# Other start places within 256 bytes for the split tokens of each layer norm

## The chip, the cores and the metric

The kernel runs on one core of a Trainium2 chip. The metric is the device time of one execution in microseconds (us); lower is better.

## The reference, cut to what matters

Two post-norm decoder layers over 256 tokens of width 2048, all in float32. Layer 0 mixes tokens with sliding-window attention (window 128, sinks, relative-position bias), layer 1 with forgetting attention; after each mixer comes a gated MLP of width 5632 with a causal convolution of width 3.

```python
def reference(x, ...):
    for i in range(DEPTH):                       # DEPTH = 2
        y = swa_sink_attention(...) if i % 2 == 0 else forgetting_attention(...)
        x = layer_norm(ALPHA * x + y, ln_g[i, 0], ln_b[i, 0])
        y = conv_ffn(x, ffn_w_up[i], ffn_conv_w[i], ffn_conv_b[i], ffn_w_down[i])
        x = layer_norm(ALPHA * x + y, ln_g[i, 1], ln_b[i, 1])
    return x

def conv_ffn(x, w_up, conv_w, conv_b, w_down):
    h = x @ w_up
    h = lax.conv_general_dilated(h, ...) + conv_b
    g, u = h[..., :D_FF], h[..., D_FF:]
    return (jax.nn.silu(g) * u) @ w_down
```

The change touches nothing of what is computed.

## The kernel before, in words

**The products.** Every large product is made of three matmuls in the rounded float32 form: both operands are split into a rounded high part and a low remainder, and high by low, low by high and high by high are added up in PSUM. Tokens in turned form (128 of the 2048 features on the partitions, 256 tokens along the row) lie in `xh` (high) and `xl` (low), 16 tiles of 1024 bytes a partition each. Weights come in chunks of 128x1024 through a ring of four: SyncE issues the load into `raw`, ScalarE copies it into `w_hi` (L473), VectorE subtracts into `w_lo` (L751), TensorE uses it.

**Two forms.** `turned_product` (L1171 to L1183) keeps 128 weight columns stationary and moves the 256 tokens of a row of `xh` or `xl` past them: its three matmuls are L1178 (`w_lo`, moving `xh`), L1180 (`w_hi`, moving `xl`) and L1181 (`w_hi`, moving `xh`), for four groups of columns. `turned_first` (L1185, matmuls L1191) does the same for the first row after a layer norm. `product` (L1155 to L1169, matmuls L1164 to L1166) keeps 128 tokens stationary and moves 512 weight columns. The turned form makes queries, keys and the up projections; the other form makes the values, the output projections (from `oh`, `ol`) and the down projections (from `hid_h`, `hid_l`). The decay gate of layer 1 has a product of its own at L1414 to L1416: 32 weight columns of `wf_lo` or `wf_hi` stationary, `xh` or `xl` moving.

**Order of the stages.** Mixer 0 (keys and values first, then four groups of queries with attention woven in), output projection, layer norm, MLP 0 (11 pairs of up projections, then down), layer norm, mixer 1 (four groups of queries, keys and values), output projection, layer norm, MLP 1, last layer norm. The instruction streams of all engines are written out by hand; semaphores tie them. `xh` and `xl` are written four times, once for each index `xi`: 0 is the input (used by mixer 0), 1 the norm before MLP 0, 2 the norm before mixer 1, 3 the norm before MLP 1. `xt_turn` (transposes L1255 and L1260 with `ident` moving) brings a tile into PSUM, `xt_evacuate` of ScalarE (L505, L508, L523) writes `xh`, and `xt_evacuate` of VectorE (L783, L786, L792) writes `xl`. `keep_clock` (L1239) is a run of matmuls of `ident` with itself that bridges each norm. No DMA reads or writes `xh` or `xl`.

**Where tiles lie.** SBUF tiles lie one behind another in the order of their allocation, each start rounded up to a multiple of 32 bytes. `res`, `raw`, `w_hi`, `w_lo`, `tok`, `cg`, `cu`, `xh`, `xl`, `oh`, `ol`, `bias`, `qT`, `kz`, `vv`, `prob`, `hid_h` and `hid_l` all start at a multiple of 256 bytes, so each row of `xh` and `xl` (1024 bytes) and each column group of `w_hi` and `w_lo` (512 bytes) does too. Some tiles do not: `ident` starts 128 bytes past a multiple of 256; `wf`, `wf_hi` and `wf_lo` start 192 bytes past one; the nine `fs` tiles of the decay (`fs0` to `fs8`) start 224 bytes past one. `xh` starts at byte 104448 of the partition, `xl` at 120832. `lnfull`, the scales of the last norm, lies on the same bytes as `xh`; `xh_hold` reserves them.

Of the kernel before, what the change touches and what calls it, by code (L numbers as in the profile page):

```python
# [22 lines left out]
F32R = mybir.dt.float32r  # L23
# [3 lines left out]
P = 128  # L27
D = 2048
SEQ = 256
MT = SEQ // P  # L30
DEPTH = 2
HD = 64
HEADS = D // HD
# [5 lines left out]
KT = D // P  # L39
# [20 lines left out]
KC = KT // 2  # L60
FC = FT // 2
CH_A_KV = 0
# [12 lines left out]
TURN_A_KV = 0  # L75
# [48 lines left out]
def trunk(nc, x, a_w_qkv, a_w_o, a_sinks, rel_bias, b_w_qkvf, b_f_bias, b_w_o,  # L124
          ffn_w_up, ffn_conv_w, ffn_conv_b, ffn_w_down, ln_g, ln_b, out):
    ctx = ExitStack()
    with ctx:
        def sb(name, shape, dt=FP32, where=ctx):
            return where.enter_context(nc.sbuf_tensor(name, shape, dt))
# [25 lines left out]
        convcol = sb("convcol", [P, DEPTH, 4, 2 * FT])  # L155
        sb("fill_to_xh", [P, 320])
        with ExitStack() as first:
            xh = sb("xh", [P, KT, SEQ], F32R, first)
        with ExitStack() as later:
            lnfull = sb("lnfull", [P, 2, D], FP32, later)  # L160
        xh_hold = sb("xh_hold", [P, KT * SEQ])
        xl = sb("xl", [P, KT, SEQ], F32R)
        with ExitStack() as mix:
            oh = sb("oh", [P, KT, SEQ], F32R, mix)
            ol = sb("ol", [P, KT, SEQ], F32R, mix)
# [20 lines left out]
            cumq = sb("cumq", [P, MT, HEADS], FP32, mix)  # L186
        hid_h = sb("hid_h", [P, FT, SEQ], F32R)
        hid_l = sb("hid_l", [P, FT, SEQ], F32R)
        ps = ctx.enter_context(nc.psum_tensor("ps", [P, 8, COLS], FP32))
        S_BANK, O_BANK, PT_BANK, X_BANK = 4, 6, 7, 4  # L190
        FIRST_BANK, AGAIN_BANK = X_BANK + 3, X_BANK + 2
# [13 lines left out]
        v_tile0 = sem("v_tile0")  # L205
# [250 lines left out]
        def _(act):  # L456
# [39 lines left out]

            def xt_evacuate(xi, l, s, g):

                if xi == 0:
                    act.wait_ge(xt_turned, g + 1)  # L500
                    src = ps[:, X_BANK + g % 4, :].rearrange("p (a t) -> p a t", a=2)
                else:
                    if g == 0:
                        act.wait_ge(first_turned, xi)
                        act.activation(xh[:, 0, :], ps[:, FIRST_BANK, 0:SEQ], ACT.Identity,  # L505
                                       scale=lncol[:, 0, l, s, 0:1], bias=lncol[:, 1, l, s, 0:1]).then_inc(first_high, 1)
                        act.wait_ge(xt_turned, KC * xi + 1)
                        act.activation(xh[:, 1, :], ps[:, X_BANK, SEQ:2 * SEQ], ACT.Identity,  # L508
                                       scale=lncol[:, 0, l, s, 1:2], bias=lncol[:, 1, l, s, 1:2]).then_inc(xt_high, 1)
                        return  # L510
                    src = cg[:, 2 * (g % 2):2 * (g % 2) + 2, :]
                    if g in DVE_FULL:
                        act.wait_ge(xt_full, FULLS * (xi - 1) + DVE_FULL.index(g) + 1)
                    else:

                        act.wait_ge(xt_low, KC * xi + g - 1)
                        act.wait_ge(xt_turned, KC * xi + g + 1)
                        for a in range(2):
                            k = 2 * g + a
                            last = act.activation(cg[:, 2 * (g % 2) + a, :], ps[:, X_BANK + g % 4, a * SEQ:(a + 1) * SEQ],  # L520
                                                  ACT.Identity, scale=lncol[:, 0, l, s, k:k + 1], bias=lncol[:, 1, l, s, k:k + 1])
                        own.link(last)
                act.activation(xh[:, 2 * g:2 * g + 2, :], src, ACT.Copy).then_inc(xt_high, 1)  # L523
# [216 lines left out]
        def _(dve):  # L740
# [33 lines left out]

            def xt_evacuate(xi, l, s, g):

                if xi == 0:
                    src = ps[:, X_BANK + g % 4, :].rearrange("p (a t) -> p a t", a=2)
                elif g == 0:
                    first_tile(xi, l, s, 0)  # L780
                    dve.wait_ge(first_full, xi)
                    dve.wait_ge(first_high, xi)
                    dve.tensor_tensor(xl[:, 0, :], cg[:, 0, :], xh[:, 0, :].bitcast(FP32), ALU.subtract).then_inc(first_low, 1)  # L783
                    first_tile(xi, l, s, 1)
                    dve.wait_ge(xt_full, FULLS * (xi - 1) + 1)
                    dve.tensor_tensor(xl[:, 1, :], cg[:, 1, :], xh[:, 1, :].bitcast(FP32), ALU.subtract).then_inc(xt_low, 1)  # L786
                    return
                else:
                    src = cg[:, 2 * (g % 2):2 * (g % 2) + 2, :]
                high = xh[:, 2 * g:2 * g + 2, :].bitcast(FP32)  # L790
                dve.wait_ge(xt_high, KC * xi + g + 1)
                dve.tensor_tensor(xl[:, 2 * g:2 * g + 2, :], src, high, ALU.subtract).then_inc(xt_low, 1)  # L792
# [363 lines left out]
        def _(pe):  # L1156
            def product(s, turn, k, nk, lh, ll, slot, tile0=None, tiles=range(MT)):
# [10 lines left out]
                        last.then_inc(tile0, 1)  # L1168
                return last  # L1169

            def turned_product(s, turn, k, slot):  # L1171

                for j in range(4):
                    if k == 0 and j % 2 == 0:
                        pe.wait_ge(acc_free[s][j // 2], turn)
                    cols = slice(j * P, (j + 1) * P)
                    o = ps[:, 2 * s + j // 2, (j % 2) * SEQ:(j % 2 + 1) * SEQ]
                    pe.matmul(o, w_lo[:, slot, k % 2, cols], xh[:, k, :], start=(k == 0 and j % 2 == 0), stop=False,  # L1178
                              skip_group_check=True)
                    pe.matmul(o, w_hi[:, slot, k % 2, cols], xl[:, k, :], start=False, stop=False, skip_group_check=True)  # L1180
                    last = pe.matmul(o, w_hi[:, slot, k % 2, cols], xh[:, k, :], start=False, stop=(k == KT - 1),  # L1181
                                     skip_group_check=True)
                return last  # L1183

            def turned_first(s, turn, slot, xi):  # L1185

                def parts(w, xs, start=False):
                    for j in range(4):
                        if start and j % 2 == 0:
                            pe.wait_ge(acc_free[s][j // 2], turn)  # L1190
                        pe.matmul(ps[:, 2 * s + j // 2, (j % 2) * SEQ:(j % 2 + 1) * SEQ], w[:, slot, 0, j * P:(j + 1) * P],  # L1191
                                  xs[:, 0, :], start=start and j % 2 == 0, stop=False, skip_group_check=True)
                pe.wait_ge(first_high, xi)
                parts(w_lo, xh, True)
                parts(w_hi, xh)
                pe.wait_ge(first_low, xi)
                parts(w_hi, xl)
# [15 lines left out]
                        last.then_inc(chunks_used, 1)  # L1213
                    yield k

            def group(s, turn, b4, loc0, lh=xh, ll=xl, nk=KT, before=None, tile0=None):

                for k in range(nk):
                    loc = loc0 + k // 2
                    if k % 2 == 0:  # L1220
                        if before:
                            before(k // 2)
                        pe.wait_ge(low_ready, b4 * 4 + (loc + 1))
                    if tile0 is last_tile0 and k >= nk - 2:

                        if k == nk - 1:
                            for m in range(MT):
                                for kk in (k - 1, k):
                                    last = product(s, turn, kk, nk, lh, ll, loc % RING, tile0, (m,))
                    else:  # L1230
                        last = product(s, turn, k, nk, lh, ll, loc % RING, tile0)
                    if k % 2 == 1:
                        last.then_inc(chunks_used, 1)
                    yield k
# [29 lines left out]
            def x_ready(xi):  # L1264
                def before(c):
                    if c == 0:
                        keep_clock(1.7 if xi == 0 else 3.4)
                        xt_turn(xi, 0)
                        xt_turn(xi, 1)
                        if xi:  # L1270
                            return
                    pe.wait_ge(xt_low, KC * xi + c + 1)
                return before
# [84 lines left out]
                    yield slot  # L1358

            def mixer_a():  # L1360
                for k in group(0, TURN_A_KV, CH_A_KV // 4, 0, before=x_ready(0)):
                    x_next(0, k)
                for k in turned_group(1, TURN_A_Q[1], CH_A_Q // 4, 0):
                    if k == 1:
# [26 lines left out]

            def mixer_b():
                t0, t1 = TURN_B

                def woven(k, n):

# [6 lines left out]
                def turn(n, b4, first=False):  # L1403
# [14 lines left out]
                    for k in turned_group(1, n + t1, b4, KC):  # L1418
                        if first and k == 12:
# [2 lines left out]
                                last = pe.transpose(ps[:, 7, m * HEADS:(m + 1) * HEADS], fs[7][:, m * P:(m + 1) * P],  # L1422
                                                    ident[0:HEADS, 0:HEADS])
                            last.then_inc(cum_turned, 1)
                    for k in group(0, n * 2 + (t0 + 1), b4, 2 * KC, tile0=v_tile0):
                        pass

                turn(0, CH_B // 4, first=True)
# [10 lines left out]

            def mlp(l):  # L1440
                t0, t1 = TURN_UP[l]

                def turn(n, b4, first=False):
                    for k in turned_group(0, n + t0, b4, 0, before=x_ready(1 + 2 * l) if first else None,
# [9 lines left out]
                with pe.Fori(0, OUT_GROUPS // 2) as n:  # L1454
                    for i in range(2):
                        for k in group(i, n + TURN_DOWN[l][i], n * (2 * FC // 4) + CH_DOWN[l] // 4, i * FC, hid_h, hid_l, FT,
                                       tile0=last_tile0 if i == 1 else None,
                                       before=lambda c: pe.wait_ge(hid_low, UP_PAIRS * (l + 1) - (1 if c < FC - 2 else 0))
# [37 lines left out]
```

## Time and profile before

| what | value |
|---|---|
| median of 2 runs | 2239.07 us (2239.05 to 2239.08) |
| profiled execution, its own time | 2239.63 us |
| its span, first to last instruction | 2237.8 us |
| TensorE matmuls busy | 2207.8 us (99%), 15265 matmuls |
| VectorE, ScalarE, GpSimd busy | 1337.7, 1038.4, 217.1 us |
| mean DMA rate | 183 GB/s |

The profiled execution lasts 1.8 us longer than its span. Busy time of TensorE counts matmuls that overlap once. Two matmuls that follow each other overlap in the profile, so the time that one costs is read from the distance of two starts, or from the busy time of a stretch divided by its matmuls, and not from its own duration.

### The profile page before, as it was taken

The page shows a single profiled execution, that of the slowest core. Times are in us where ns is not written, and L with a number is a line of the kernel's source. Part 1 is how long each engine was busy: PE and PEld are TensorE (multiplying, and loading weights), DVE is VectorE, ACT ScalarE, POOL GpSimd, SP SyncE. Part 2 cuts the span into 40 slices and gives each one's busy share as a digit, 9 for nine tenths or more (in the row PEclk, how much of TensorE's full clock was granted, in tenths as well). Part 3 has the DMA queues.
Part 4 walks back from the last instruction along what each step waited for, and adds up shares of the span by engine and source line. Part 5 has one row for each costly group of instructions (what it writes and reads, how often), then busy time and mean ns, then how long its engine had stood idle before and what let it go on. Part 6 is the DMA issues. An engine that isn't in the chain of part 4 may idle for free.

```text
span 2237.8 us, 40894 instructions
## 1 busy us (share of the span) xinstructions
PE 2207.8 (99%) x15265; PEld 2061.6 (92%) x15265; DVE 1337.7 (60%) x1805; ACT 1038.4 (46%) x1380; POOL 217.1 (10%) x206
## 2 busy tenths in 40 slices
PE   9999999999999999999999999999999999999996
PEld 8998899999999988888999998899999999988885
DVE  5566676665666554546665565576666566554445
ACT  4554464454444443335444444364444444443332
POOL 2000002220000000000240330001230000000001
PEclk9999999999999999999999999999999999999998
DMA  8444556666666666655655654656666666666653
GB/s 263 148 147 159 178 170 198 190 194 182 183 180 185 179 193 192 195 190 163 189 182 163 201 169 141 204 155 196 193 199 182 180 185 179 185 225 191 194 193 109
DMA packets 206953, 408.71 MB, mean 183 GB/s; under 512 B 12653, under 2 KB 13757, under 8 KB 206621
## 3 DMA queue, kind: packets, MB, share of 16 engines
q1 hardware_dynamic: 200192, 385.92, 56.8%
q0 software_dynamic: 5776, 21.34, 3.0%
q8 instruction: 49, 0.80, 0.1%
q10 hardware_dynamic: 908, 0.43, 0.1%
q14 instruction: 28, 0.22, 0.0%
HBM read 405.46 MB, written 2.18 MB: 182 GB/s over the span
## 4 chain that ended last, share of the span: by engine, by line
PE 96%; DVE 3%; ACT 0%; issue 0%; DMA 0%; DVEq 0%; ACTq 0%
PE ps L1178 19%; PE ps L1181 19%; PE ps L1180 19%; PE ps L1164 11%; PE ps L1166 11%; PE ps L1165 11%; PE ps L1306 1%; PE ps L1313 1%; PE ps L1325 1%; PE ps L1324 1%; PE ps L1305 1%; DVE w_lo L751 1%; PE ps L1323 0%; PE ps L1255 0%; DVE cg L796 0%
## 5 line engine op out<-in xcount | busy, mean ns | idle before, releaser
L751 DVE TENSOR_TENSOR w_lo<-raw,w_hi 128x1024 fp32r<-128x1024 f32 x728 | 922.5, 1273 | 672.7 <-ACT w_hi L473 671.1
L473 ACT ACTIVATE w_hi<-raw 128x1024 fp32r<-128x1024 f32 x728 | 770.3, 1058 | 999.7 <-PE ps L1181 582.5
L1178 PE MATMUL ps<-xh,w_lo 128*128 128x256 f32 x3572 | 1020.0, 286 | 2.5 <-DVE xl L792 1.5
L1181 PE MATMUL ps<-xh,w_hi 128*128 128x256 f32 x3572 | 1010.6, 283 | 0.0
L1180 PE MATMUL ps<-xl,w_hi 128*128 128x256 f32 x3572 | 1010.5, 283 | 0.0
L1178 PEld LDWEIGHTS ps<-xh,w_lo 128*128 128x128 f32 x3572 | 685.0, 192 | 5.4 <-DVE xl L792 2.9
L1180 PEld LDWEIGHTS ps<-xl,w_hi 128*128 128x128 f32 x3572 | 685.2, 192 | 0.3
L1181 PEld LDWEIGHTS ps<-xh,w_hi 128*128 128x128 f32 x3572 | 685.0, 192 | 0.0
L1164 PE MATMUL ps<-w_lo,hid_h 128*128 128x512 f32 x704 | 273.9, 389 | 0.0
L1165 PE MATMUL ps<-w_hi,hid_l 128*128 128x512 f32 x704 | 273.9, 389 | 0.0
L1166 PE MATMUL ps<-w_hi,hid_h 128*128 128x512 f32 x704 | 273.9, 389 | 0.0
L1166 PEld LDWEIGHTS ps<-w_hi,hid_h 128*128 128x128 f32 x704 | 132.1, 188 | 27.7
L1165 PEld LDWEIGHTS ps<-w_hi,hid_l 128*128 128x128 f32 x704 | 132.1, 188 | 27.3
L1164 PEld LDWEIGHTS ps<-w_lo,hid_h 128*128 128x128 f32 x704 | 132.1, 188 | 27.2
L395 POOL COPY cw<-convcol 128x16 f32 (+1 forms) x40 | 41.9, 1048 | 801.8 <-DVE cu L1080 441.3
L1164 PE MATMUL ps<-w_lo,oh 128*128 128x512 f32 x256 | 102.4, 400 | 0.0
L1166 PE MATMUL ps<-w_hi,oh 128*128 128x512 f32 x256 | 99.9, 390 | 0.0
L1165 PE MATMUL ps<-w_hi,ol 128*128 128x512 f32 x256 | 99.7, 390 | 0.0
L1080 DVE SCALAR_TENSOR_TENSOR cu<-ps,cw,cu 128x254 f32<-128x254 f32 (+1 forms) x176 | 76.6, 477 | 1.6
L1080 DVE SCALAR_TENSOR_TENSOR cg<-ps,cw,cg 128x254 f32<-128x254 f32 (+1 forms) x176 | 76.5, 476 | 1.6
L1164 PE MATMUL ps<-w_lo,xh 128*128 128x512 f32 x160 | 63.7, 398 | 2.6 <-issue 2.6
L1165 PE MATMUL ps<-w_hi,xl 128*128 128x512 f32 x160 | 63.1, 394 | 0.0
(164 smaller groups left out, 1497.1 us busy)
## 6 DMA issues: line engine op xcount, KB each, us to landing
raw<-in_ffn_w_up_dram SPq DMA_DIRECT2D x352, 512.0 KB, 3.6
raw<-in_ffn_w_down_dram SPq DMA_DIRECT2D x176, 512.0 KB, 4.6
raw<-in_b_w_qkvf_dram SPq DMA_DIRECT2D x96, 512.0 KB, 4.4
raw<-in_a_w_qkv_dram SPq DMA_DIRECT2D x40, 512.0 KB, 4.4
raw<-in_a_w_o_dram SPq DMA_DIRECT2D x32, 512.0 KB, 4.3
raw<-in_b_w_o_dram SPq DMA_DIRECT2D x32, 512.0 KB, 4.6
bias<-rel_by_distance POOLq DMA_DIRECT2D x4, 1024.0 KB, 6.4
bias<-minus_cumulated_decay POOLq DMA_DIRECT2D x4, 1024.0 KB, 6.4
```

The source lines that it names most:

```text
L395: gp.tensor_copy(cw[:, h], convcol[:, l, :, bass.ds(n * 4 + h * FT, 4)]).then_inc(cw_ready, 1)
L473: act.activation(w_hi[:, loc % RING], raw[:, loc % RING], ACT.Copy).then_inc(high_ready, 1)
L751: dve.tensor_tensor(w_lo[:, s], raw[:, s], w_hi[:, s].bitcast(FP32), ALU.subtract).then_inc(low_ready, 1)
L1080: last = dve.scalar_tensor_tensor(dst[:, j, lag:SEQ], src, cw[:, h, tap, j:j + 1], dst[:, j, lag:SEQ], ALU.mult, ALU.add)
L1164: pe.matmul(o, lh[:, k, rows], w_lo[:, slot, k % 2, :], start=(k == 0), stop=False)
L1165: pe.matmul(o, ll[:, k, rows], w_hi[:, slot, k % 2, :], start=False, stop=False)
L1166: last = pe.matmul(o, lh[:, k, rows], w_hi[:, slot, k % 2, :], start=False, stop=(k == nk - 1))
L1178: pe.matmul(o, w_lo[:, slot, k % 2, cols], xh[:, k, :], start=(k == 0 and j % 2 == 0), stop=False, skip_group_check=True)
L1180: pe.matmul(o, w_hi[:, slot, k % 2, cols], xl[:, k, :], start=False, stop=False, skip_group_check=True)
L1181: last = pe.matmul(o, w_hi[:, slot, k % 2, cols], xh[:, k, :], start=False, stop=(k == KT - 1), skip_group_check=True)
L1305: pe.matmul(o[:, 0:P], qT[:, s // 2, 0:P], kz[:, kt, s % 2, 0:P], start=True, stop=True)
L1306: pe.matmul(o[:, P:SPAN], qT[:, s // 2, P:SEQ], kz[:, kt, s % 2, :], start=True, stop=True).then_inc(scores_ready, 1)
```

## The change

`xh` and `xl` become 256 bytes longer, and each layer norm's tokens start at a place of their own in them: 48, 8, 32 and 16 elements, which is 192, 32, 128 and 64 bytes, for `xi` 0, 1, 2 and 3. Both tiles use the same place for one `xi`. Every reader and writer takes the view of its `xi`. The rows keep their distance of 1024 bytes, so each row of one `xi` starts at the same place within 256 bytes. `xl` moves up by 256 bytes and all tiles behind it by 512. The number, order and shape of the instructions and their waits stay.

```diff
@@ -28,6 +28,10 @@
 MT = SEQ // P
+
+
+PLACES = (48, 8, 32, 16)
+PLACED = D // P * SEQ + 64
 DEPTH = 2
@@ -155,11 +159,11 @@
         with ExitStack() as first:
-            xh = sb("xh", [P, KT, SEQ], F32R, first)
+            xh_all = sb("xh", [P, PLACED], F32R, first)
         with ExitStack() as later:
             lnfull = sb("lnfull", [P, 2, D], FP32, later)
-        xh_hold = sb("xh_hold", [P, KT * SEQ])
-        xl = sb("xl", [P, KT, SEQ], F32R)
+        xh_hold = sb("xh_hold", [P, PLACED])
+        xl_all = sb("xl", [P, PLACED], F32R)
@@ -186,6 +190,7 @@
+        xhs, xls = ([t[:, at:at + KT * SEQ].rearrange("p (k t) -> p k t", t=SEQ) for at in PLACES] for t in (xh_all, xl_all))
@@ -496,6 +501,7 @@
             def xt_evacuate(xi, l, s, g):
 
+                xh = xhs[xi]
@@ -774,6 +780,7 @@
             def xt_evacuate(xi, l, s, g):
 
+                xh, xl = xhs[xi], xls[xi]
@@ -1168,7 +1175,11 @@
+            layer = [0]
+
             def turned_product(s, turn, k, slot):
+
+                xh, xl = xhs[layer[0]], xls[layer[0]]
@@ -1183,6 +1194,8 @@
             def turned_first(s, turn, slot, xi):
+
+                xh, xl = xhs[xi], xls[xi]
@@ -1213,7 +1226,7 @@
-            def group(s, turn, b4, loc0, lh=xh, ll=xl, nk=KT, before=None, tile0=None):
+            def group(s, turn, b4, loc0, lh, ll, nk=KT, before=None, tile0=None):
@@ -1358,7 +1371,7 @@
-                for k in group(0, TURN_A_KV, CH_A_KV // 4, 0, before=x_ready(0)):
+                for k in group(0, TURN_A_KV, CH_A_KV // 4, 0, xhs[0], xls[0], before=x_ready(0)):
@@ -1391,6 +1404,8 @@
             def mixer_b():
                 t0, t1 = TURN_B
+                layer[0] = 2
+                xh, xl = xhs[2], xls[2]
@@ -1422,7 +1437,7 @@
-                    for k in group(0, n * 2 + (t0 + 1), b4, 2 * KC, tile0=v_tile0):
+                    for k in group(0, n * 2 + (t0 + 1), b4, 2 * KC, xh, xl, tile0=v_tile0):
@@ -1439,6 +1454,7 @@
             def mlp(l):
                 t0, t1 = TURN_UP[l]
+                layer[0] = 1 + 2 * l
```

## Rows read from the trace of the kernel before

**Rows 1.** The page: span, busy time of the engines, granted clock in 40 slices.

```profile
span 2237.8 us, 40894 instructions
PE 2207.8 (99%) x15265; PEld 2061.6 (92%) x15265; DVE 1337.7 (60%) x1805; ACT 1038.4 (46%) x1380; POOL 217.1 (10%) x206
...
PEclk9999999999999999999999999999999999999998
```

**Rows 2.** The page: the chain that ended last, by engine.

```profile
PE 96%; DVE 3%; ACT 0%; issue 0%; DMA 0%; DVEq 0%; ACTq 0%
```

**Rows 3.** Stretches: stretch, busy us and count of each engine, granted clock, DMA share.

```profile
36.90:172.60 135.70, 135.70 (x1122) 133.45 (x1120) 82.39 (x211) 67.40 (x166) 5.27 (x6) 1.00 0.52 162
...
274.20:282.30 8.10, 7.29 (x48) 6.28 (x46) 6.87 (x21) 4.28 (x9) 0.33 (x2) 1.00 0.05 18
282.30:790.60 508.30, 507.75 (x4232) 507.35 (x4230) 323.12 (x383) 253.26 (x297) 52.98 (x44) 1.00 0.64 186
790.60:1030.00 239.40, 239.40 (x1059) 198.21 (x1058) 120.25 (x111) 97.41 (x94) 0.00 (x0) 1.00 0.61 193
...
1038.10:1360.70 322.60, 320.81 (x2312) 301.74 (x2311) 199.47 (x308) 151.54 (x240) 82.63 (x54) 1.00 0.59 182
...
1470.20:1978.50 508.30, 507.75 (x4231) 507.35 (x4230) 321.72 (x383) 253.23 (x297) 53.13 (x44) 1.00 0.64 186
```

**Rows 4.** Instruction groups: count | busy us, mean ns | idle before, releaser.

```profile
L1178 PE MATMUL ps<-xh,w_lo 128*128 128x256 f32 x3572 | 1020.0, 286 | 2.5 <-DVE xl L792 1.5 <-DVE vv L1043 0.9
...
L473 ACT ACTIVATE w_hi<-raw 128x1024 fp32r<-128x1024 f32 x728 | 770.3, 1058 | 999.7 <-PE ps L1181 582.5 <-PE ps L1166 374.2 <-DMA raw<-in_ffn_w_down_dram 16.0
...
L1164 PE MATMUL ps<-w_lo,xh 128*128 128x512 f32 x160 | 63.7, 398 | 2.6 <-issue 2.6
...
L1191 PE MATMUL ps<-xh,w_lo 128*128 128x256 f32 x12 | 2.1, 300 | 0.0
```

**Rows 5.** Timeline, mixer 1: start us, us; weights at 0, then at 192.

```profile
1062.15 0.28 PE L1178 MATMUL ps<-xh,w_lo 128*128 128x256 f32 x1
...
1062.27 0.28 PE L1180 MATMUL ps<-xl,w_hi 128*128 128x256 f32 x1
...
1062.51 0.28 PE L1414 MATMUL ps<-xh,wf_lo 128*32 128x256 f32 x1
...
1062.63 0.28 PE L1415 MATMUL ps<-xl,wf_hi 128*32 128x256 f32 x1
...
1063.19 0.28 PE L1414 MATMUL ps<-xh,wf_lo 128*32 128x256 f32 x1
```

**Rows 6.** Timeline of TensorE: plain float32 matmuls, `kz` (0) or `ident` (128) moving.

```profile
71.67 0.60 PE L1306 MATMUL ps<-kz,qT 128*128 128x256 f32 x2
...
274.24 3.62 PE L1239 MATMUL ps<-ident 128*128 128x256 f32 x16
```

**Rows 7.** Those two lines by themselves: count: duration ns min/median/max.

```profile
L1306 PE MATMUL ps<-kz,qT x128: 379/380/382, 67.5 to 1385.2; 128*128 128x256 f32 x128
...
L1239 PE MATMUL ps<-ident x56: 377/379/796, 1.5 to 1465.4; 128*128 128x256 f32 x56
```

**Rows 8.** Instruction groups, columns as Rows 4: the same work at 0, 192 and 224.

```profile
L792 DVE TENSOR_TENSOR xl<-cg,xh 128x512 fp32r<-128x512 f32 x21 | 14.5, 690 | 5.4 <-ACT xh L523 5.2
...
L523 ACT ACTIVATE xh<-cg 128x512 fp32r<-128x512 f32 x21 | 13.3, 633 | 14.2 <-DVE cg L796 13.9
...
L783 DVE TENSOR_TENSOR xl<-cg,xh 128x256 fp32r<-128x256 f32 x3 | 1.3, 425 | 0.1
...
L1049 DVE TENSOR_TENSOR wf_lo<-wf,wf_hi 128x512 fp32r<-128x512 f32 x1 | 0.7, 687 | 0.0
...
L638 ACT ACTIVATE wf_hi<-wf 128x512 fp32r<-128x512 f32 x1 | 0.6, 615 | 0.0
...
L1029 DVE TENSOR_TENSOR fs<-fs 32x256 f32<-32x256 f32 x1 | 0.4, 416 | 0.0
```

## The prediction

> **What bounds the kernel now.** I read the page first. Matmuls fill 2207.8 of the 2237.8 us of the span, the granted clock is at 0.9 or more in 39 of the 40 slices, and no other engine passes 60% [rows 1]. The chain that ended last is TensorE for 96% of the span [rows 2]. The groups say why the others are idle: of the 999.7 us that ScalarE sat idle before its copies into `w_hi`, 956.7 us were ended by a matmul that gave back a ring slot [rows 4]. The weights are ready early and the split engines wait for TensorE. So the time is the sum of matmuls times what each costs, and the change can only matter through (a) the cost of a matmul that reads `xh` or `xl`, (b) the writes of these tiles in the norms, (c) anything that the move of the other tiles does.
>
> The cost of a matmul comes from the stretches. The up projections of MLP 0 hold 4232 matmuls in 507.75 us, which is 0.1200 us each; those of MLP 1 give 507.75 / 4231 = 0.1200 as well. The down projections hold 1059 in 239.40 us, 0.2261 each [rows 3]. A moving row of 256 columns costs 0.1200 and one of 512 costs 0.2261, so 256 columns more cost 0.1061 us and the fixed part of a turned matmul is 0.1200 - 0.1061 = 0.0139 us. I keep 0.0139 as the piece of each turned matmul that does not stream columns.
>
> **The change part by part.**
>
> The moving reads. Each of L1178, L1180 and L1181 has 3572 matmuls, and L1191 has 12 for each of its three operand pairs (the one row shown has 12), so 3 x 3584 = 10752 turned matmuls move a row of `xh` or `xl` [rows 4]. By the loops they fall on the places as: 768 at 192 bytes (mixer 0), 4224 at 32 bytes (MLP 0), 1536 at 128 bytes (mixer 1) and 4224 at 64 bytes (MLP 1). 48 more are those of the decay gate, at 128 bytes. The trace has no matmul of the rounded form whose moving row starts off a multiple of 256 bytes, so the cost must be bounded.
>
> - Nearest row for "nothing": a 256-column matmul in plain float32 that moves `ident`, 128 bytes past a multiple of 256, against one that moves `kz`, at a multiple. Sixteen of the first last 3.62 us, one alone 0.379, so the pace is (3.62 - 0.38) / 15 = 0.216 us; two of the second last 0.60, so 0.60 - 0.38 = 0.22 us [rows 6, 7]. The same columns and weights, another place, the same pace to the rounding of the row. It reads a column in twice the time of the rounded form (0.216 against 0.120), so it leaves room to hide a small cost, and does not settle the case.
> - Lower end: the decay gate's matmuls move `xh` at the same pace of columns and run at (1063.19 - 1062.51) / 6 = 0.1133 us, against 0.120 just before them [rows 5]. Their stationary operand starts at 192 bytes and has 32 columns, not 128. If it is the place that helps, a turned matmul could fall by 0.0067 us: 10752 x 0.0067 = 72 us less.
> - Upper end: the plain float32 pace of 0.216 [rows 6], as if an odd start halved the read: 10752 x 0.096 = 1032 us more.
>
> Between ends so far apart I take zero, by the `ident` row, which is the only one that changes the place of a moving operand and little else.
>
> A rule bears on this. The Trainium skill (SBUF — State Buffer, Specifications) says that SBUF is read in lines of 16 bytes and that crossing to a new line is what costs. All four places are multiples of 16, so a row of 1024 bytes stays at 64 lines, and by that page the term is zero too; a place of 8 bytes would be another matter. No row here shows the line size.
>
> The stationary reads. 480 matmuls of the other form (three lines of 160, the first shown) take 128 tokens of `xh` or `xl` as weights while `w_lo` or `w_hi` moves, and these still move from a multiple of 256 [rows 4]. Stationary operands at an odd place are shown: `wf_lo` and `wf_hi` at 192, with no sign of a price (0.1133, below the usual pace) [rows 5]. I take zero; even the whole fixed part again, 480 x 0.0139, would be 6.7 us.
>
> The writes. ScalarE's and VectorE's evacuations of `xh` and `xl` have twins in the trace that work on `wf`, `wf_hi` and `wf_lo` at 192 bytes, with the same shape and types: 615 ns against 633 for ScalarE, 687 against 690 for VectorE; a two-input VectorE operation on 256 columns takes 416 ns on `fs` at 224 bytes (on 32 partitions) and 425 at a multiple of 256 [rows 8]. So an odd place costs these engines nothing to 0.02 us. There are 29 evacuations of each kind of 512 columns, and all but the first of each norm lie beside matmuls of the norm; the bridge of a norm is 8.1 us long with 7.29 us of matmuls in it [rows 3]. Taken at the largest difference seen, 0.018 us, two evacuations on the path of each of four fillings come to 0.14 us, either way. I take zero.
>
> The move of the other tiles. `xl` moves by 256 bytes, what lies behind it by 512. Each tile keeps its place within 256 bytes. The instructions, their order and waits are the same, so no queue and no wait changes. Zero. `lnfull` shares `xh`'s bytes as before and is loaded after the last up projection.
>
> The sum: 0 + 0 + 0 + 0. Against the profiled execution (span 2237.8, its own time 2239.63) that is 2239.6 us. The runs without a profile have a median of 2239.07, 0.56 below it, and agree within 0.03, so I predict 2239.1 us.
>
> **The rivals.**
>
> Slower: a block more for each moving row. A row of 1024 bytes that starts at a multiple of 256 lies in four blocks of 256 bytes; at any of the four new places it lies in five. If TensorE fetches by such blocks, the fifth takes the time of 64 columns, 0.1061 / 4 = 0.0265 us. Part of it may fit in the fixed 0.0139 us, where no columns stream; the rest, 0.0126, or with a less lucky overlap the 0.0139 again, is paid by each of 10752 matmuls: 10752 x 0.0139 = 149 us, which gives 2388.6 us. In full it would be 285 us, 2524 us. The point from which this decides is 44.8 us (2%, about what a measurement of this kernel can tell from no change) over 10752 matmuls, 0.0042 us each: ten columns' time. For it: every moving row of the rounded form now starts at a multiple, so the trace cannot deny it, and the read runs at twice the pace of plain float32. Against: L1239 reads the 512 bytes of `ident` twice from 128, each time three blocks in place of two, and shows nothing. The Trainium skill (DMA: Bandwidth & Descriptors, How a descriptor splits into AXI transactions) has just this rule of 256-byte blocks, but for a DMA; no DMA touches these tiles, and nothing here shows that TensorE follows it.
>
> Slower at one place alone. If blocks are of 64 bytes, only 32 is off (MLP 0): 4224 x 0.0139 = 59 us, 2297.8 us. If 192 bytes alone is bad, mixer 0 pays 768 x 0.0139 = 10.7 us, 2249.8 us, which is within 2%.
>
> Faster: a clash goes. The fixed part could be two reads, weights and tokens, that begin on the same place within 256 bytes; the matmuls with weights at 192 are 0.0067 quicker. All turned matmuls would have them apart after the change: 2239.1 - 72 = 2167 us. For it: the numbers just named. Against: those also load 32 columns of weights instead of 128, which explains a shorter fixed part as well; and `ident` loads and moves from the same place (128) at the pace of `kz` and `qT` [rows 6], while a clash should hit the former no less. In mixer 0 alone it would be 768 x 0.0067 = 5.1 us, 2234.0 us.
>
> The change does not do what it says: if the places ended up all alike within 256 bytes, the time stays, which can't be told from the forecast by time alone.
>
> **How the numbers follow.** No effect beyond 0.1%, 0.84. The fifth block in all layers 0.04; a price at one or two places of over 2% in total 0.02; a price at some place within 2% 0.04; the clash gone in all layers 0.03, in part 0.03 (of which 0.01 beyond 2%). Faster by over 2%: 0.04. Slower by over 2%: 0.06. Within 2%: 0.90. The range reaches to the two partial cases of mixer 0, 2234 below and 2250 above; beyond it lie the full rivals, and what they leave out is under 2 in 10.
>
> **What would show it.** Right: 4232 matmuls of MLP 0 in 507.8 us and the like number of MLP 1 in the same time, 0.1200 each, the down projections at 0.2261, evacuations at 633 and 690 ns. The fifth block: up projections at 0.134 or more, all alike in layers 0 and 1, down projections unchanged. One place: the stretches of mixer 0, MLP 0, mixer 1 and MLP 1 come out with different costs per matmul; that is what makes this change easy to read, since each has a place of its own. The clash: 0.113 in the turned form. If TensorE's pace stays and the time moves, the norms' bridges (8.1 us) have grown, and I mis-sized the writes.

## The result, and the profile after

The change takes the median from 2239.07 to 2213.94 us (2213.89 and 2213.99 in two runs): a ratio of 0.9888, 95% interval 0.9845 to 0.9930. It is faster, by 1.1%: clear of the noise, though within 2%, and outside the range, whose lower end was 2234. The profiled execution has a span of 2212.1 us against 2237.8, so 25.7 us less.

The page of the kernel after the change, its span, busy times, granted clock and last chain (lines of the code have moved: L1178, L1180, L1181 are now L1189, L1191, L1192; L1164 to L1166 are L1171 to L1173; L473 is L478):

```profile
span 2212.1 us, 40894 instructions
PE 2182.2 (99%) x15265; PEld 2033.5 (92%) x15265; DVE 1335.3 (60%) x1805; ACT 1039.1 (47%) x1380; POOL 217.7 (10%) x206
...
PEclk9999999999999999999999999999999999999998
...
PE 96%; DVE 3%; ACT 0%; DMA 0%; issue 0%; SPq 0%; ACTq 0%; DVEq 0%
```

Against [rows 1, 2] the instructions and the clock are the same, TensorE is still on 96% of the chain, and VectorE, ScalarE and GpSimd are busy within 2.4 us of what they were. TensorE's rows are what changed: its matmuls are busy for 25.6 us less, which is all of the gain, and its weight loads (PEld) for 28.1 us less. The stretches of the same stages say in which of them (the columns of [rows 3]):

```profile
36.60:169.30 132.70, 132.70 (x1122) 130.37 (x1120) 82.37 (x211) 67.31 (x166) 5.27 (x6) 1.00 0.52 166
...
270.90:279.00 8.10, 7.26 (x48) 6.26 (x46) 6.87 (x21) 4.27 (x9) 0.33 (x2) 1.00 0.06 24
279.00:773.40 494.40, 493.78 (x4231) 493.38 (x4229) 322.57 (x383) 253.58 (x297) 52.83 (x44) 1.00 0.65 191
773.40:1012.80 239.40, 239.40 (x1058) 198.23 (x1057) 120.21 (x111) 97.41 (x94) 0.00 (x0) 1.00 0.61 193
...
1020.90:1344.30 323.40, 321.91 (x2314) 300.75 (x2313) 197.07 (x308) 151.60 (x240) 82.60 (x54) 1.00 0.59 182
...
1453.70:1952.80 499.10, 498.50 (x4232) 498.10 (x4230) 322.74 (x383) 253.57 (x297) 53.99 (x44) 1.00 0.65 189
```

The up projections of MLP 0 (tokens at 32 bytes) lose 13.9 us, those of MLP 1 (64 bytes) 9.2 us, mixer 0 (192 bytes) 3.0 us, and mixer 1 (128 bytes) gains nothing: it is 0.8 us longer. The norm's bridge (8.1 us) and the down projections (239.4 us) are where they were. Per matmul, MLP 0 is at 493.78 / 4231 = 0.1167 us and MLP 1 at 498.50 / 4232 = 0.1178, against 0.1200 in both before.

The groups show that the engines that write these tiles did not feel the places (633 and 690 ns, as in [rows 8]), and that ScalarE's wait for ring slots got shorter by as much as TensorE did (999.7 us before, 974.2 now):

```profile
L1189 PE MATMUL ps<-xh,w_lo 128*128 128x256 f32 x3572 | 1007.2, 282 | 2.2 <-DVE xl L799 1.6
...
L478 ACT ACTIVATE w_hi<-raw 128x1024 fp32r<-128x1024 f32 x728 | 771.2, 1060 | 974.2 <-PE ps L1192 557.6 <-PE ps L1173 375.6 <-DMA raw<-in_ffn_w_down_dram 15.5
...
L799 DVE TENSOR_TENSOR xl<-cg,xh 128x512 fp32r<-128x512 f32 x21 | 14.5, 690 | 5.4 <-ACT xh L529 5.2
...
L529 ACT ACTIVATE xh<-cg 128x512 fp32r<-128x512 f32 x21 | 13.3, 633 | 14.2 <-DVE cg L803 13.9
```

So a turned matmul became cheaper, by an amount that depends on where the tokens start. Why the start should matter, and the start against what, is what the experiments were for.

### The profile page after: what moved, and what is told of

The parts are those of the page before. It is cut to its first block, busy times and chain, and to the rows that moved or that the text cites. A ratio compares the mean times of both kernels' runs of the same rounds, so it can differ in the third digit from the quotient of the medians.

```text
span 2212.1 us, 40894 instructions
## 1 busy us (share of the span) xinstructions
PE 2182.2 (99%) x15265; PEld 2033.5 (92%) x15265; DVE 1335.3 (60%) x1805; ACT 1039.1 (47%) x1380; POOL 217.7 (10%) x206
## 4 chain that ended last, share of the span: by engine, by line
PE 96%; DVE 3%; ACT 0%; DMA 0%; issue 0%; SPq 0%; ACTq 0%; DVEq 0%
PE ps L1192 19%; PE ps L1189 19%; PE ps L1191 19%; PE ps L1171 11%; PE ps L1173 11%; PE ps L1172 11%; PE ps L1319 1%; PE ps L1326 1%; PE ps L1338 1%; PE ps L1337 1%; PE ps L1318 1%; PE ps L1336 0%; DMA raw<-in_a_w_qkv_dram 0%; DVE cg L803 0%; PE ps L1345 0%; PE ps L1268 0%
## 5 line engine op out<-in xcount | busy, mean ns | idle before, releaser
L478 ACT ACTIVATE w_hi<-raw 128x1024 fp32r<-128x1024 f32 x728 | 771.2, 1060 | 974.2 <-PE ps L1192 557.6
L1189 PE MATMUL ps<-xh,w_lo 128*128 128x256 f32 x3572 | 1007.2, 282 | 2.2 <-DVE xl L799 1.6
L1192 PE MATMUL ps<-xh,w_hi 128*128 128x256 f32 x3572 | 999.0, 280 | 0.0
L1191 PE MATMUL ps<-xl,w_hi 128*128 128x256 f32 x3572 | 997.4, 279 | 0.0
L1189 PEld LDWEIGHTS ps<-xh,w_lo 128*128 128x128 f32 x3572 | 670.7, 188 | 5.2 <-DVE xl L799 3.0
L1191 PEld LDWEIGHTS ps<-xl,w_hi 128*128 128x128 f32 x3572 | 672.0, 188 | 0.4
L1192 PEld LDWEIGHTS ps<-xh,w_hi 128*128 128x128 f32 x3572 | 671.4, 188 | 0.0
L1171 PE MATMUL ps<-w_lo,hid_h 128*128 128x512 f32 x704 | 273.9, 389 | 0.0
L1173 PE MATMUL ps<-w_hi,hid_h 128*128 128x512 f32 x704 | 273.9, 389 | 0.0
L1173 PEld LDWEIGHTS ps<-w_hi,hid_h 128*128 128x128 f32 x704 | 132.2, 188 | 27.4
L1171 PEld LDWEIGHTS ps<-w_lo,hid_h 128*128 128x128 f32 x704 | 132.2, 188 | 27.4
L1171 PE MATMUL ps<-w_lo,oh 128*128 128x512 f32 x256 | 102.4, 400 | 0.0
L1173 PE MATMUL ps<-w_hi,oh 128*128 128x512 f32 x256 | 99.9, 390 | 0.0
L1171 PE MATMUL ps<-w_lo,xh 128*128 128x512 f32 x160 | 64.2, 401 | 3.1 <-issue 2.6
L1173 PE MATMUL ps<-w_hi,xh 128*128 128x512 f32 x160 | 63.6, 398 | 0.0
```

Source lines behind the costliest of these rows:

```text
L478: act.activation(w_hi[:, loc % RING], raw[:, loc % RING], ACT.Copy).then_inc(high_ready, 1)
L1171: pe.matmul(o, lh[:, k, rows], w_lo[:, slot, k % 2, :], start=(k == 0), stop=False)
L1173: last = pe.matmul(o, lh[:, k, rows], w_hi[:, slot, k % 2, :], start=False, stop=(k == nk - 1))
```

## The experiments

Each kernel is the changed one with other places. `xh` and `xl` get places of their own, and where weights move too, `w_hi` and `w_lo` become 256 bytes longer and begin at a place as well, with the filler ahead of `xh` shortened by the 512 bytes of both (128 elements), so that `xh` and what lies behind it stay:

```diff
-PLACES = (48, 8, 32, 16)
+XH_PLACES = (...)
+XL_PLACES = (...)
+WH_PLACE, WL_PLACE = ...
-        w_hi = sb("w_hi", [P, RING, 2, COLS], F32R)
+        w_hi = sb("w_hi", [P, RING * 2 * COLS + 64], F32R)[:, WH_PLACE:WH_PLACE + RING * 2 * COLS].rearrange("p (r k c) -> p r k c", r=RING, k=2)
... (the same for w_lo, with WL_PLACE)
-        sb("fill_to_xh", [P, 320])
+        sb("fill_to_xh", [P, 320 - 128])
```

The places in the code count elements of 4 bytes; the text gives bytes. Two theories stand against each other. R: the pace of a turned matmul is set by the distance, within 256 bytes, between the moving tokens' start and the start of the weights that are loaded beside them. M: it is set by the tokens' own place.

The pace is read from a stretch of 400 us inside the up projections of each MLP. A stretch of length T in which the matmuls, 0.28 us long, follow each other at a pace p holds (T + 0.28) / p of them, so p = 400.28 / count. For 200 us of the down projections, where a matmul lasts 0.39 us, it is 200.39 / count. These are rows of a view of stretches, with TensorE alone: stretch, busy us (count), granted clock, DMA share, GB/s.

**e1, the places undone, the longer tiles kept.**

```diff
-PLACES = (48, 8, 32, 16)
+XH_PLACES = (0, 0, 0, 0)
+XL_PLACES = (0, 0, 0, 0)
```

> Tiles longer by 256 bytes as in the change, everything behind them moved by 256 and 512 bytes, but all four norms' tokens at place 0. Theory R (the pace of a turned matmul is set by where the moving row starts against where the weights being loaded start) and theory M (it is set by the moving row's own place): both 0.1200 us per turned matmul in every layer and 2239 us, within 1. Rival S (what gained was the move of the other tiles, not the places): 2214 us.

```profile
300.00:700.00 400.00, 400.00 (x3336) 1.00 0.65 189
...
1520.00:1920.00 400.00, 400.00 (x3335) 1.00 0.65 187
```

2239.48 us (10 runs), ratio 1.0001 (0.9991 to 1.0010). 400.28 / 3336 = 120.0 ns. The move of the other tiles is worth nothing; the rival S (that this move made the gain) is out, and the whole gain is the places'.

**e2, one of the two token tiles at 32 bytes.**

```diff
+XH_PLACES = (8, 8, 8, 0)
+XL_PLACES = (8, 0, 8, 8)
```

> One of the two token tiles keeps place 0: in MLP 0 xh at 32 bytes and xl at 0, in MLP 1 xh at 0 and xl at 32; both at 32 in the two mixers. If each matmul pays for its own moving row (R and M alike), MLP 0, with two of three rows at 32, has (2 x 116.7 + 120.0) / 3 = 117.8 ns and MLP 1, with one of three, 118.9 ns; 2222 us or so. If what counts is that xh and xl lie at the same or at different places (theory H, the hand-over from one moving row to the next), the two MLPs come out alike.

2214.77 us. MLP 0 held 3399 matmuls, 117.8 ns, as forecast; MLP 1 held 3420, 117.0 ns, where 118.9 was forecast: with only one moving row of three off the weights, MLP 1 gained more than with two of three. The two MLPs are not alike, so H (what counts is whether `xh` and `xl` share a place) as stated is out, and so is the notion that each matmul simply pays for its own row. The pace seems to be one of the whole repeated pattern, not a sum over its rows.

**e3, weights at 32 bytes.**

```diff
+XH_PLACES = (0, 8, 0, 0)
+XL_PLACES = (0, 8, 0, 0)
+WH_PLACE, WL_PLACE = 8, 8
```

> w_hi and w_lo start 32 bytes past a multiple of 256 in tiles 256 bytes longer; tokens at 32 in MLP 0 and at 0 in MLP 1 and both mixers. R: MLP 0, where tokens and weights are again at one place, goes back to 120.0 ns; MLP 1, with the two 32 apart, leaves 120; about 14 us of the gain of MLP 0 gone. M: MLP 0 116.7 ns as after the change, MLP 1 120.0. In the down projections (weights moving at 32, tokens stationary at 0): R and M both allow another pace than the 226.7 ns of before; if it stays, that form doesn't feel the place of what it moves.

```profile
300.00:700.00 400.00, 400.00 (x3336) 1.00 0.65 189
800.00:1000.00 200.00, 200.00 (x859) 1.00 0.59 188
1520.00:1920.00 400.00, 400.00 (x3382) 1.00 0.66 190
```

2250.44 us, slower than the kernel before. In MLP 0 tokens and weights both start at 32 and the pace is back at 120.0 ns, to the matmul the count of e1; in MLP 1 tokens at 0 now run at 118.4, where tokens at 0 had never left 120. M is refuted on both sides: the tokens' own place does not set the pace alone. The down projections went from 884 matmuls in 200 us to 859, from 226.7 to 233.3 ns: that form pays for this distance, where the turned form gains.

**e4 to e6, other places with the weights at 0.** Places in bytes in the order mixer 0, MLP 0, mixer 1, MLP 1: e4 has 224, 128, 96, 192; e5 has 32, 16, 192, 224; e6 has 128, 96, 64, 160.

> Other places, the same for xh and xl: 224 bytes in mixer 0, 128 in MLP 0, 96 in mixer 1, 192 in MLP 1. R and M: each place has a pace of its own whatever the layer, so MLP 0 gets near the 118.8 ns that mixer 1 showed at 128, and MLP 1 near the 115.4 ns that mixer 0 showed at 192, some 10 us faster than at 64. If the paces belong to the layers and not to the places, MLP 0 keeps 116.7 and MLP 1 117.8.

> Places scanned again, the same for xh and xl: 32 bytes in mixer 0, 16 in MLP 0, 192 in mixer 1, 224 in MLP 1. R (the distance between the tokens' and the weights' place counts): MLP 1 has the distance that weights at 32 with tokens at 0 had, so 118.3 ns; 16 bytes in MLP 0 is new: between 116.7 and 120.0 if the effect is smooth in the place, 120.0 if it goes by whole blocks of 32 bytes. The decay gate's matmuls have weights at 192 and now tokens at 192: if the clash is one of equal places it shows there for the first time, at over 113.3 ns; if it comes from the length of the load of 128 columns, they stay at 113.3.

> 128 bytes in mixer 0, 96 in MLP 0, 64 in mixer 1, 160 in MLP 1. R and M: MLP 0 near the 119.9 ns of mixer 1 at 96, mixer 1 near the 117.8 of MLP 1 at 64; 160 is new, between the 118.7 at 128 and the 117.7 at 192. The sum over the layers is about 2228 us.

e4: 2226.50 us; 128 gives 118.7 ns in MLP 0, near the 118.8 that it had in mixer 1, but 192 gives 117.8 in MLP 1 and not the 115.4 of mixer 0 (the paces of the mixers are mean distances of the starts of turned matmuls that follow each other, attention's left out). So the place decides in the first pair and not in the second. Within mixer 0 of the changed kernel the mean pace at 192 bytes moves too: 113.5, 115.1, 117.2 and 115.3 ns in its four quarters. e5: 2199.39 us; 224 gives 118.3, within 0.1 of what weights at 32 with tokens at 0 gave in e3, which is the same distance within 256 bytes. And 16 bytes gives 113.3 ns, the lowest of all. e6: 2226.79 in the profiled execution, with 96 back at 120.0 and 160 at 117.3 (between 117.7 and 118.7 was forecast), but 2232.0 and 2232.7 in two more; the forecast 2228 lay between, and why the executions differ no profile shows; e15 has a cause that may do it.

e5 also answers the question on the decay gate, whose weights (at 192, 32 columns) and tokens (at 192) had one place for the first time. Its `wf_lo` row, count: duration min/median/max, first and last start:

```profile
L1430 PE MATMUL ps<-xh,wf_lo x16: 276/276/279, 1032.7 to 1037.8; 128*32 128x256 f32 x16
```

Sixteen rows of three matmuls, 45 steps in 5.1 us: 113 ns, as before the change at a distance. So an equal place did not slow these few matmuls with a load of 32 columns, where the large products with a load of 128 run at 120.0 at equal multiples of 32. (The large products were never run with both at 192.) The short load is not free of the place either: with tokens at 32 (e7) the same 45 steps took 5.3 us, about 117 ns each.

**e7, the best of the places seen by then**: 192, 32, 32, 32 bytes.

> The best place seen so far in each layer: 192 bytes in mixer 0, 32 in MLP 0, mixer 1 and MLP 1. R and M alike, from the paces seen: MLP 1 gains 4224 x (117.8 - 116.7) = 4.6 us on the change, mixer 1 1536 x (118.8 - 116.9) = 2.9, less 0.2 for its matmuls with stationary tokens: 2206.5 us, below both kernels.

2207.08 us (2206.98 to 2207.54), ratio 0.9856 (0.9840 to 0.9873); MLP 0 held 3430 matmuls and MLP 1 3431, 116.7 ns each. The sum of the paces was right to 0.6 us.

**e8, w_lo alone at 32 bytes**, tokens at 0, in MLP 1 at 32.

> w_lo alone starts at 32 bytes, w_hi stays at 0; tokens at 0 in all but MLP 1, where they are at 32. R: in MLP 0 one load of three lies apart from the tokens, near 118.9 ns, in MLP 1 two of three, near 117.8. M: 120.0 and 116.7. In the down projections one moving row of three is 32 bytes off the stationary tokens: (2 x 226.7 + 233.3) / 3 = 228.9 ns by R, which is 2112 x 2.2 ns = 4.6 us more.

```profile
800.00:1000.00 200.00, 200.00 (x859) 1.00 0.59 188
...
1980.00:2180.00 200.00, 200.00 (x867) 1.00 0.59 191
```

2234.29 us (2234.0 to 2236.7 in eight executions). MLP 0 118.3 ns (3383), MLP 1 117.0 (3421). The down projections ran at 233.3 ns (859) in MLP 0 and at 231.1 (867) in MLP 1, though their operands lie at the same places in both: here one set of places has two paces within one execution. All 1056 of one MLP at 2.2 ns more would be 2.3 us, about what the slowest two executions lie above the others; they were not profiled. Neither theory's number: R was nearer in MLP 0 (118.9), M in MLP 1 (116.7). One load of three off the tokens at 0 did in MLP 0 what three of three did in e3 (118.4), and one moving tile of two off did to the down projections of MLP 0 what both did there (233.3, with 228.9 forecast). Adding up the matmuls of the pattern does not work here either.

**e9, all tokens at 16 bytes.**

> All four norms' tokens 16 bytes past a multiple of 256. R and M alike: each turned matmul at the 113.4 ns that MLP 0 showed, so from the scan with 16 in MLP 0 and 224 in MLP 1: MLP 1 gains 4224 x (118.3 - 113.4) = 20.7 us, the mixers some 768 x 3 + 1536 x 2.4 = 6 us, if the matmuls with stationary tokens don't lose it: 2173 us. If the pace belongs to the layer, MLP 1 stays over 116.

```profile
300.00:700.00 400.00, 400.00 (x3532) 1.00 0.68 199
...
1470.00:1870.00 400.00, 400.00 (x3373) 1.00 0.65 189
```

A median of 2193.74 us, ratio 0.9771 (0.9728 to 0.9814), but the four executions read 2176.1, 2190.0, 2197.5 and 2197.8. In the profiled one (2197.8), the same place ran at 113.3 ns in MLP 0 and at 118.7 in MLP 1, both held through all of the 400 us. The forecast of 2173 was wrong for this execution and about right for the quickest. The matmuls with stationary tokens ran at 16 bytes as at 0: 90 of them in 20 us of mixer 1, as before the change, where the changed kernel (128 bytes) has 87.

**e10, weights at 16 bytes**, tokens at 0, 16, 0, 32.

> w_hi and w_lo start 16 bytes past a multiple of 256; tokens at 0 in both mixers, 16 in MLP 0, 32 in MLP 1. R: MLP 0 (distance 0) 120.0 ns, MLP 1 (distance 16) 113.4. M: MLP 0 113.4, MLP 1 116.7. The down and output projections move weights at 16 past stationary tokens at 0: if their clash were of the same kind as in the turned form they would fall below 226.7; if any distance hurts them, they go to about 233 as with 32.

```profile
300.00:700.00 400.00, 400.00 (x3382) 1.00 0.66 191
800.00:1000.00 200.00, 200.00 (x865) 1.00 0.60 189
1520.00:1920.00 400.00, 400.00 (x3335) 1.00 0.65 187
```

2245.03 us (one of eight executions at 2234.5). R fails here: equal places at 16 give 118.4 and not 120.0, and 16 apart gives 120.0 and not 113.3. M fails as well. The down projections, 16 bytes off, ran at 231.7 ns: slower than 226.7, and less so than at 32. R was drawn from places that are multiples of 32, and that is where it may hold.

**e11, 8 and 48 bytes** in MLP 0 and MLP 1, 240 and 80 in the mixers.

> 240 bytes in mixer 0, 8 in MLP 0, 80 in mixer 1, 48 in MLP 1. If the lines that matter are 16 bytes long and odd numbers of lines apart are good, 48, 80 and 240 give some 113.4 ns and 8 does not (a moving row then starts within a line): 120 or worse. If only small distances are good, 8 gives 113 to 117, and 48 lies above 116.7.

2217.58 us. 8 bytes gives 116.7 ns (3431) and 48 gives 118.3 (3383). Neither reading held: an 8 is no worse than a 32, and 48 is not quick.

**e12, weights at 64 bytes**, tokens at 16, 96, 112, 128.

> w_hi and w_lo at 64 bytes; tokens at 16 in mixer 0, 96 in MLP 0, 112 in mixer 1, 128 in MLP 1. R, restricted to places that are multiples of 32: MLP 0 (32 apart) at 116.7 ns, where weights at 0 gave 120.0 for the same place 96; MLP 1 (64 apart) at 117.8, where weights at 0 gave 118.7 for 128. M: 120.0 and 118.7. The down projections (64 apart the other way) stay at about 233.

```profile
300.00:700.00 400.00, 400.00 (x3431) 1.00 0.67 194
800.00:1000.00 200.00, 200.00 (x875) 1.00 0.61 192
1520.00:1920.00 400.00, 400.00 (x3399) 1.00 0.66 190
```

2221.86 us. 3431 and 3399 are the very counts that 32 and 64 bytes gave with the weights at 0 in the changed kernel. With the weights at 0, 96 and 128 bytes had given 120.0 and 118.7. So among multiples of 32 the distance decides in all four cases that were tried with the weights at two places: 0 apart (e1, e3), 32 and 64 apart (the changed kernel, e12) and 224 apart (e5, e3). The down projections came out at 229.0 ns, better than the 233 forecast and worse than 226.7.

**e13 and e14, odd multiples of 16**: 112, 80, 176, 240 and 144, 112, 48, 208.

> Odd multiples of 16: 112 bytes in mixer 0, 80 in MLP 0, 176 in mixer 1, 240 in MLP 1; weights at 0. If the quick pace of 113.3 ns belongs to odd multiples of 16 in general, at least one of the two MLPs shows it; if it belongs to 16 alone, both lie between 116 and 120 as 48 did (118.3).

> Odd multiples of 16 again: 144 bytes in mixer 0, 112 in MLP 0, 48 in mixer 1, 208 in MLP 1; weights at 0. Same readings as for 80 and 240. Between 113.3 and 120 ns everywhere; a steady pace below 116.7 that two executions share would be a better place than 32.

e13: 2217.6 and 2224.5 us; 80 gives 120.0 ns (3336) and 240 gives 117.1 (3417); the two executions lie 6.9 us apart, and no profile shows why. e14: 2207.8 and 2208.3 us; 112 gives 113.3 (3532), 208 gives 119.2 (3359). So the quick pace belongs neither to 16 alone nor to odd multiples of 16 in general.

**e15, the kernel of e9 again, for its executions.**

> The kernel with all tokens at 16 once more, for its executions. If each MLP settles by chance at its entry into one of two paces, 113.3 or 118.7 ns, the times of the executions form groups about 4224 x 5.3 ns = 22.5 us apart: some 2175, 2197 and, with both MLPs slow, 2220 us, and the profiled execution shows one pace through all turns of an MLP, not necessarily 113.3 in MLP 0 and 118.7 in MLP 1 as the last time. If the pace belongs to the MLP, MLP 0 is at 113.3 and MLP 1 at 118.7 again.

```profile
300.00:700.00 400.00, 400.00 (x3532) 1.00 0.68 199
...
1470.00:1870.00 400.00, 400.00 (x3532) 1.00 0.68 198
```

The executions read 2175.9, 2176.2, 2176.6, 2190.0, 2198.3 and 2212.6 us; the profiled one is the first, and has 113.3 ns in both MLPs. Beside e9 this shows it: the same program, the same place, and MLP 1 at 118.7 ns in one execution and 113.3 in the other; the two executions lie 2197.8 - 2175.9 = 21.9 us apart, and 4224 x 5.34 ns = 22.6. The times about 2190 and that of 2212.6 were in no profile, and what made them stays open; the forecast groups (2175, 2197, 2220) don't hold them.

**e16, both MLPs and mixer 0 at 112 bytes, mixer 1 at 16.**

> Tokens at 112 bytes in mixer 0 and both MLPs, at 16 in mixer 1; weights at 0. If 112 bytes gives the quick pace in each execution, 8448 x 3.2 ns under the kernel with 32 bytes in the MLPs, with the mixers a little quicker too: 2175 us, all executions within 1 us of each other. If 112 has two paces as 16 has, the times fall into groups again, from 2175 to some 2215 us, and 32 bytes stays the best place of which each execution gives the same.

```profile
300.00:700.00 400.00, 400.00 (x3532) 1.00 0.67 199
...
1470.00:1870.00 400.00, 400.00 (x3532) 1.00 0.67 198
```

2174.66 us (2174.21 to 2175.34 in five executions), ratio 0.9711 (0.9697 to 0.9724): 39 us below the changed kernel, and all executions alike. This version beats both kernels.

All paces of the turned form with the weights at 0, from the MLPs, most of them from one profiled execution. Since 16 bytes has two, a difference between two places seen once each is not yet a property of the places:

| tokens' place, bytes | 0 | 8 | 16 | 32 | 48 | 64 | 80 | 96 | 112 | 128 | 160 | 192 | 208 | 224 | 240 |
|---|---|---|---|---|---|---|---|---|---|---|---|---|---|---|---|
| matmuls in 400 us | 3336 | 3431 | 3532 or 3373 | 3431 | 3383 | 3399 | 3336 | 3335 | 3532 | 3373 | 3412 | 3399 | 3359 | 3383 | 3417 |
| ns of one | 120.0 | 116.7 | 113.3 or 118.7 | 116.7 | 118.3 | 117.8 | 120.0 | 120.0 | 113.3 | 118.7 | 117.3 | 117.8 | 119.2 | 118.3 | 117.1 |

The place before, 0, shares the highest of them, with 80 and 96.

## Why the prediction was wrong

**What bounds the kernel** held. TensorE's matmuls set the time before and after, and the up projections' gain in pace times their number gives the gain of the stretch: 4224 x 3.3 ns = 13.9 us in MLP 0. The fixed part was a little too large: 239.40 / 1059 counts matmuls that only reach into the stretch, and 200.39 / 884 gives 226.7 ns, so 106.7 ns for 256 columns more and 13.3 ns fixed, not 13.9. The prices of the slower rivals go down by 4% with it, which changes nothing else.

**The moving reads** are the step that failed: "Between ends so far apart I take zero, by the `ident` row, which is the only one that changes the place of a moving operand and little else." Two things are wrong with it. The first is what the row compares: in L1239 `ident` is loaded and moved from the same place, 128 and 128; in L1306 `qT` is loaded from 0 and `kz` moved from 0 [rows 6]. The distance is zero in both, and the distance is what e3 and e12 showed to count among multiples of 32. I had written down that `ident` meets itself, and used it against the clash as if that were a test of it. The second is the form. The trace before also has plain float32 rows with the two apart, which the prediction didn't look at: `ident` moves from 128 while `prob` or `res`, at a multiple of 256, is loaded.

```profile
72.10 0.49 PE L1313 MATMUL ps<-ident,prob 128*128 128x128 f32 x3
...
278.87 0.82 PE L1255 MATMUL ps<-ident,res 128*128 128x128 f32 x6
```

One of them lasts 0.273 us, so their pace is (0.49 - 0.273) / 2 = 0.109 and (0.82 - 0.273) / 5 = 0.109 us for 128 columns. `ident` past itself takes 0.216 for 256, or 0.108 for 128. In plain float32 a distance of 128 bytes gains nothing that these rows can show (other distances have no row), while in the rounded form it gains 1.3 ns of 120. So even the right comparison in that form would have said zero, and carrying zero from plain to rounded float32 was the step without support; the caution beside it, that the slower form leaves room to hide a small cost, was noted and then set aside. What the runs showed in place of zero is -3.3 ns at 32 bytes, -2.2 at 64, -1.3 at 128 and some -4 at 192 (3.0 us over 768), in all about 28 us, less some 3 us that the stationary reads cost.

Of the rivals the clash, with a chance of 0.06, pointed the right way, and what it hangs on, the places of weights and tokens against each other, is shown by e3 and e12. As a rule (only equal places are slow) it fails: equal places at 16 gave 118.4 ns and 16 apart from them 120.0 (e10), and tokens 80 or 96 bytes from the weights gave 120.0, as at 0. Its price was mis-sized as well. The 6.7 ns of the decay gate is the most that any place gave (113.3, at 16 and 112), but the four places chosen give a fifth to some two thirds of it. "All turned matmuls would have them apart after the change: 2239.1 - 72 = 2167 us" took the full price for any distance; e16, at places picked for it, gets to 2174.66. The other objection, that the gate's load is only 32 columns long, may be half right: in e5 the short load was not slowed by an equal place. But 128 columns reach 113.3 ns too, at 16 and 112 bytes, so the short load is not needed for that pace.

**The rule on lines of 16 bytes** ("by that page the term is zero too"; the Trainium skill, SBUF — State Buffer, Specifications) led nowhere. Places 32, 64 and 128 are whole lines and have three paces, and 8 bytes, which cuts a line, is as good as 32 (e11). A second rule was not weighed and should have been, for it is the one that spoke for zero: the Trainium skill (TensorE: Matmul & The Clock Gate, Part 2: What happens when you issue a matmul) says that "Loading the next tile's weights doesn't steal SBUF read bandwidth from the running matmul." In the rounded float32 form the measurement does not agree that the two leave each other alone: moving the weights' tile by 32 bytes with the tokens at 0 (e3) changes the pace from 120.0 to 118.4 ns in the turned form and from 226.7 to 233.3 in the other. Whether it is bandwidth that is lost, and whether the load or the matmul is held up, no run shows.

**The slower rivals** (a fifth block, 64-byte blocks, a price at 192 alone) are refuted: no place gave an MLP a pace above 120.0, and mixer 0, at 192, is 3.0 us shorter.

**The stationary reads** were taken as zero and cost something: with tokens at 128 bytes, 87 matmuls of mixer 1 in 20 us against 90, 234 against 227 ns, or 384 x 8 ns = 3 us at most. It outweighs the 1536 x 1.3 ns = 2.0 us that the turned matmuls of mixer 1 gained, so that stage is 0.8 us longer.

**The writes and the moved tiles** were right: 690 ns again, 8.1 us of bridge again, and e1 at a ratio of 1.0001, with all places back at 0.

**The range** left out too little below. The lower end was computed, 72 us, from a real row; the range stopped at 2234 because only mixer 0 was let in. That the change stayed within 2%, which had a chance of 0.90, came true by luck of the places chosen and not by the reason given: with others (e16) the kernel is 2.9% faster.

What stays open: why 16 bytes has two paces and 112 has shown one, why 80 and 96 bytes are as slow as 0, and what in the memory the distance acts on. That the load of the next weights meets the moving row fits that both places count (e3, e8, e12), but it does not foretell e10, and nothing here looks inside the memory. The two paces at one place, held through a whole loop, look like a pattern that locks in when the loop is entered; that was not tested.

## What to carry to other kernels

When TensorE bounds a kernel in a form whose pace has a fixed part (here 120.0 ns for 256 columns, of which by the estimate above 106.7 go with the columns), try the places of the moving and the stationary tile within 256 bytes against each other; it costs a few hundred bytes and was worth 2.9% here (e16). Measure each place by the pace inside a long loop, in more than one execution, and give each form its own place: the form with 512 moving columns was quickest (226.7 ns) with both at 0, and as quick with its stationary tokens at 16. And before a row is used as proof of "no effect", ask whether it changes the one thing that the effect would hang on, and whether it is of the same form.

## What the runs showed of the hardware that was not expected

- A turned matmul (128 columns loaded, 256 moved, rounded float32) takes 113.3 to 120.0 ns by the places of its operands, at the same clock and with the same neighbours.
- Among the multiples of 32 bytes tried only the distance counts: tokens and weights at 0 and 0 or at 32 and 32, 3336 matmuls in 400 us; 32 and 0 or 96 and 64, 3431; 64 and 0 or 128 and 64, 3399; 224 and 0, 3383, or 0 and 32, 3382. At 16 bytes this fails (e10).
- The prices of single matmuls don't add up: one tile of four moved changes the mean pace by 1.7 to 3.0 ns (e2, e8), against 3.3 for both token tiles moved.
- The same places can have two paces, each held for a whole loop: MLP 1 at 16 bytes ran at 113.3 ns in one profiled execution and at 118.7 in another (2175.9 and 2197.8 us), and the down projections of e8 at 233.3 ns in MLP 0 and 231.1 in MLP 1 of one execution.
- With 512 moving columns a distance costs the down projections 6.6 ns at 32 bytes (226.7 to 233.3), 5.0 at 16 and 2.3 at 64; stationary tokens at 16 bytes, with the weights at 0, ran as at 0.
- In plain float32, `ident` moved from 128 past weights at 0 keeps the pace of `ident` past itself: 0.109 against 0.108 us for 128 columns.
